# Seven block products for four of the eight row tiles of the output projections behind the feed-forward

## What is computed

```
def second_block(x, ...):
    for i in range(4):                 # mla, swa, fox, mla
        o = attention_i(x)             # 512 x 1024, 16 heads of 64
        y = (o * silu(gate)) @ w_out[i]            # 1024 x 1024
        x = layernorm(8 ** 0.25 * x + y, ln_g[i], ln_b[i])
    return x
```

## Time and profile before

| | |
|---|---|
| median of 3 runs | 1786.05 us (1785.99 to 1786.71) |
| profiled execution | 1786.31 us, its span 1784.5 us |
| granted TensorE clock | 0.998 in the mean |
| DMA | 147.94 MB, 83 GB/s |

### The profile page before, as it was taken

The page is one execution under the profiler, slowest core; times in us unless marked ns, Lnnn a source line. Parts: engine busy times, 40 slices in busy tenths (PEclk is TensorE's granted clock), DMA queues, the critical chain, the costliest instruction groups (busy, mean ns, idle before and its releaser), DMA issues.

```text
span 1784.5 us, 24874 instructions
## 1 busy us (share of the span) xinstructions
PE 1763.0 (99%) x9776; PEld 1416.5 (79%) x9776; DVE 992.6 (56%) x2091; ACT 810.8 (45%) x1737; POOL 727.3 (41%) x441
## 2 busy tenths in 40 slices
PE   9999999999999999999999999999999999999997
PEld 6787877788888888889776798888877777887676
DVE  4558688564351524254777368755644342567764
ACT  5434455453342323244476344554345343446662
POOL 4534521154686868633312333234332324332122
PEclk9999999999999999999999999999999999999999
DMA  5322320153505151324212232113331222421212
GB/s 170 99 74 71 95 60 25 36 177 92 169 25 176 36 165 48 97 74 105 61 35 82 85 99 71 60 62 96 104 87 56 74 69 84 104 68 37 61 55 72
DMA packets 215032, 147.94 MB, mean 83 GB/s; under 512 B 51825, under 2 KB 197249, under 8 KB 214914
## 3 DMA queue, kind: packets, MB, share of 16 engines
q1 hardware_dynamic: 210592, 137.10, 27.2%
q10 hardware_dynamic: 4322, 9.24, 1.5%
HBM read 144.22 MB, written 2.10 MB: 82 GB/s over the span
## 4 chain that ended last, share of the span: by engine, by line
PE 89%; DVE 7%; ACT 3%; issue 1%; DMA 0%; POOL 0%; SPq 0%; DVEq 0%; ACTq 0%
PE PS L427 24%; PE PS L429 23%; PE PS L428 23%; PE PS L515 6%; PE PS L577 6%; PE PS L601 4%; PE PS L779 1%; DVE PS L1645 1%; ACT X L1172 1%; DVE X L1648 1%; DVE PS L1664 1%; PE PS L1033 1%; PE PS L802 1%; ACT Wh L1113 0%; PE PS L1054 0%
## 5 line engine op out<-in xcount | busy, mean ns | idle before, releaser
L2291 POOL TENSOR_TENSOR Wl<-Wr,Wh 128x1024 fp32r<-128x1024 f32 (+3 forms) x367 | 600.9, 1657 | 1005.4 <-ACT Wh L1113 1005.1
L427 PE MATMUL PS<-XTl,Wh 128*128 128x512 f32 (+1 forms) x1096 | 412.9, 377 | 1.0 <-DVE KF L1683 0.8
L429 PE MATMUL PS<-XTh,Wh 128*128 128x512 f32 (+1 forms) x1096 | 408.1, 372 | 0.0
L428 PE MATMUL PS<-XTh,Wl 128*128 128x512 f32 (+1 forms) x1096 | 408.0, 372 | 0.0
L1113 ACT CAST Wh<-Wr 128x1024 fp32r<-128x1024 f32 (+5 forms) x274 | 249.3, 931 | 156.9 <-PE PS L429 95.7
L427 PEld LDWEIGHTS PS<-XTl,Wh 128*128 128x128 f32 x1096 | 206.5, 188 | 45.5 <-issue 9.9
L429 PEld LDWEIGHTS PS<-XTh,Wh 128*128 128x128 f32 x1096 | 206.4, 188 | 36.4
L428 PEld LDWEIGHTS PS<-XTh,Wl 128*128 128x128 f32 x1096 | 206.5, 188 | 34.8
L427 PE MATMUL PS<-Wl,XTh 128*128 128x512 f32 (+2 forms) x608 | 227.3, 374 | 2.1 <-DVE XTl L1656 1.5
L429 PE MATMUL PS<-Wh,XTh 128*128 128x512 f32 (+2 forms) x608 | 224.1, 369 | 0.0
L428 PE MATMUL PS<-Wh,XTl 128*128 128x512 f32 (+2 forms) x608 | 223.9, 368 | 0.0
(11 more groups left out here) (342 smaller groups left out, 2749.5 us busy)
## 6 DMA issues: line engine op xcount, KB each, us to landing
Wr<-in_w_in SPq DMA_DIRECT2D x38, 512.0 KB, 3.8
Wr<-in_fox_w_in SPq DMA_DIRECT2D x32, 512.0 KB, 4.2
Wr<-in_w_ffn_gate SPq DMA_DIRECT2D x22, 512.0 KB, 4.2
Wr<-in_w_ffn_up SPq DMA_DIRECT2D x22, 512.0 KB, 4.0
Wr<-in_swa_w_in SPq DMA_DIRECT2D x20, 512.0 KB, 4.0
WP<-in_w_ffn_down SPq DMA_DIRECT2D x9, 1024.0 KB, 9.2
Wr<-in_mla_w_in SPq DMA_DIRECT2D x16, 512.0 KB, 4.2
Wr<-in_mla_w_out SPq DMA_DIRECT2D x16, 512.0 KB, 3.4
```

The costliest lines, as they stand in the source:

```text
L427: pe.matmul(o, l[0], r[1], start=start, stop=False, skip_group_check=again)
L428: pe.matmul(o, l[1], r[0], start=False, stop=False, skip_group_check=again)
L429: return pe.matmul(o, l[0], r[0], start=False, stop=stop, skip_group_check=again)
L2291: ins = raw.tensor_tensor(l[:, cs], r[:, cs], h[:, cs].bitcast(F), sub)
```

## The change

In all four stages the row tiles 0 to 3 of the output projection, as two pairs q = 0, 1 (row tiles 2q and 2q + 1), are multiplied in another way, after Strassen and Winograd. A pair is a product of a 2 x 2 block matrix of gated tiles (rows 0 to 255 and 256 to 511, two row tiles) with a 2 x 2 block matrix of weights (two row tiles, two halves of columns). It is made of seven block products in place of eight; each block product is two (v = 0, 1) for two tiles of rows, so 14 products by `mm3` and not 16.

- Weights (`sums7`, on GpSimd, ahead of the piece "even" in its order of pieces): four sums of 128 x 512. Pieces of a stage are now, in this order, even0, sums0, even1, sums1, odd0, fours (for both pairs), odd1, and row tiles 4 to 7 as they are: 11 in place of 8. ("Even" is the even row tile, its right half replaced by a sum; "sums" and "fours" are sums.) The odd row tile is loaded twice, once for the sums and once as a piece of its own: 10 loads in place of 8. ScalarE's wait for "even", "sums" and "fours" is a wait for GpSimd's sums.
- Factors (`factors`, ScalarE and VectorE): the tiles 2q, 2q + 1 of `GT` give seven factors of 128 x 256, three as they are and four sums, which VectorE makes; they are split into `FS`, 256 + 512 + 1024 columns. It stands at the step ("gate", x), with x by SEVENS: 5 and 6 in the MLA stages, 3 and 5 in fox, 2 and 4 in swa. In MLA and fox `FS` lies over buffers that are no longer needed by then. The tiles 0 to 3 are no longer split at the stage's end; "out" is left for 4 to 7.
- Products (`outproj7`): four of the seven products have banks of their own in the first pass (A, B, C, E, each for v = 0, 1; 48 matmuls for both pairs). VectorE adds each to the rows and halves of X that it belongs to (`combine`: A and B to three places, C and E to one; A's scale the residual on the way), and the second pass (36 matmuls) goes on in the banks A, C and E, where a sum started. Then the row tiles 4 to 7 follow as before, i by i, in the same banks (B's start anew). mla1 has the same order as the others.
- The ring of raw slots takes the odd row tile as an entry of its own, which is free again when GpSimd has made the fourth sum.
- At the event ("fu", 21), the last upward product of the feed-forward, two more pieces are due.

```diff
+SEVENS = {'swa': (2, 4), 'fox': (3, 5), 'mla0': (5, 6), 'mla1': (5, 6)}
...
-            if kind == "odd":
+            if kind == "odd" and c not in SEVENS:
                 return pair_in[q].at(c)
-            if kind == "ring":
+            if kind in ("ring", "odd"):
                 return raw_in[ring[i] % RAW_SLOTS].at(i)
-            return by_pool.at(kind, c, min(2 * q + 1, PAIRS - 1) if kind == "fours" else q)
+            return by_pool.at(kind, c, min(2 * q + 1, (2 if c in SEVENS else PAIRS) - 1) if kind == "fours" else q)
+        def released(entry):
+            if entry in odd_of:
+                return by_pool.at("fours", *homes[odd_of[entry]][1:])
+            return weight_lo.at(entry)
...
-                    due[signal, key] = min(count[0] + AHEAD + (key[:2] == ("swa", 1)), len(used) + W_SLOTS)
+                    due[signal, key] = min(count[0] + AHEAD + (key[:2] == ("swa", 1)) + 2 * (key == ("fu", 21)), len(used) + W_SLOTS)
...
+                        ring["odd", i] = len(ringed)
+                        ringed.append(("odd", i))
                 return i
...
+            def outproj7(s, src, lhs, ready, turned=True):
+                A, B, C, E = ([take(("y", s, v + i, c)) for v in range(2)] for i, c in ((0, 0), (2, 1), (0, 1), (2, 0)))
+                place = {(v + i, c): bs[v] for bs, i, c in ((A, 0, 0), (B, 2, 1), (C, 0, 1), (E, 2, 0)) for v in range(2)}
+                FS = O7[s][0]
+                def row(a):
+                    return [(src[:, a:a + 1, :], 0)]
+                def product(bs, v, w, h, j, q, start, stop, again=False):
+                    e.wait_ge(weight_lo.at(w), *free(bs[v]), by_dve.at("fs", s, q))
+                    return mm3(PS[bs[v]][:, :], [t[:, q, j, tile(v)] for t in FS], part(w, 0, D, 512 * h, 512 * h + 512), start, stop, again)
+                for q in range(2):
+                    w2 = weight(row(2 * q), D, ("even", s, q))
+                    odd_src[w2] = row(2 * q + 1)
+                    w13 = weight(row(2 * q), D, ("sums", s, q))
+                    for bs, w, h, j, x in ((A, w2, 0, 0, "A"), (B, w2, 1, 5, "B"), (C, w13, 0, 4, "C"), (E, w13, 1, 3, "E")):
+                        for v in range(2):
+                            ins = product(bs, v, w, h, j, q, q == 0, q == 1)
+                            if q:
+                                ins.then_inc(*done(psum_full, "part", s, x, v))
+                        if h:
+                            if not q:
+                                ins.then_inc(*weight_used.next())
+                            used[w] = psum_full.now() if q else weight_used.now()
+                for q in range(2):
+                    wo = weight(row(2 * q + 1), D, ("odd", s, q))
+                    if q == 0:
+                        w4 = weight(row(0), D, ("fours", s, 0))
+                    for bs, w, h, j, x in ((A, wo, 0, 1, "A"), (C, wo, 1, 6, "C"), (E, w4, q, 2, "E")):
+                        for v in range(2):
+                            e.wait_ge(by_dve.at("part", s, x, v))
+                            ins = product(bs, v, w, h, j, q, False, False, again=True)
+                        if h:
+                            ins.then_inc(*weight_used.next())
+                            used[w] = weight_used.now()
+                ws = [(weight(row(a), D), a) for a in range(4, 8)]
+                for i in range(NT):
+                    for c in range(2):
+                        b, fresh = place[i, c], i >= 2 and c == 1
+                        if fresh:
+                            e.wait_ge(by_dve.at("part", s, "B", i - 2))
+                        for w, a in ws:
+                            e.wait_ge(weight_lo.at(w), *ready(a))
+                            ins = mm3(PS[b][:, :], pair(lhs, ALL, a, tile(i)), part(w, 0, D, 512 * c, 512 * c + 512), fresh and a == 4, a == 7, again=not fresh)
+                            if i == NT - 1 and c == 1 and a < 7:
+                                ins.then_inc(*weight_used.next())
+                                used[w] = weight_used.now()
+                        ins.then_inc(*done(psum_full, "y", s, i, c))
+                        give(b, (by_dve, ("normed", s, i, c)))
+                    if turned and i in (1, 2):
+                        turn_tile(s, i - 1)
+                used[ws[-1][0]] = psum_full.at("y", s, NT - 1, 1)
...
+            def factors(s, q):
+                FS, _, _, S4 = O7[s]
+                g = GT[s][:, 2 * q:2 * q + 2, :].rearrange("p f (a t) -> p (f a) t", a=2)
+                e.wait_ge(by_dve.at(s, "o", 2 * q + 1), *overlaid(s, q))
+                high(FS[0][:, q, 0, :], g[:, 0, :], "fs_hi", s, q)
+                high(FS[0][:, q, 1:3, :], g[:, 2:4, :], "fs_hi", s, q)
+                e.wait_ge(by_dve.at("sf", s, q))
+                high(FS[0][:, q, 3:7, :], S4[:, :, :], "fs_hi", s, q)
...
+                    elif kind == "gate" and x in SEVENS.get(s, ()):
+                        factors(s, SEVENS[s].index(x))
+                    elif kind == "out" and (x >= 4 or s not in SEVENS):
                         gated(s, x)
...
+                for x in "ACEB":
+                    for v in range(2):
+                        b, low, right = bank[("y", s, *{"A": (v, 0), "B": (v + 2, 1), "C": (v, 1), "E": (v + 2, 0)}[x])][:, :], X[:, v + 2, HALVES[0]], X[:, v::2, HALVES[1]]
+                        e.wait_ge(psum_full.at("part", s, x, v), by_dve.now())
+                        if x in "AB":
+                            scale = ALPHA if x == "A" else 1.0
+                            ve.scalar_tensor_tensor(low, low, scale, b, mult, add).then_inc(*by_dve.next())
+                            ve.scalar_tensor_tensor(right, right, scale, b.unsqueeze(1).broadcast_to([128, 2, 512]), mult, sub).then_inc(*by_dve.next("part", s, x, v))
+                        else:
+                            y = X[:, v + 2, HALVES[1]]
+                            ve.tensor_tensor(y, y, b, add if x == "C" else sub).then_inc(*by_dve.next("part", s, x, v))
+                e.wait_ge(by_dve.now())
             def norm_tail(s, alpha=ALPHA, x_ready=lambda i: None):
+                if s in SEVENS:
+                    combine(s)
                 for i in range(NT):
...
+            def factors(s, q):
+                FS, _, _, S4 = O7[s]
+                g = GT[s][:, 2 * q:2 * q + 2, :].rearrange("p f (a t) -> p (f a) t", a=2)
+                e.wait_ge(by_dve.now(), *([by_act.at("fs_hi", s, q - 1)] if q else []), *overlaid(s, q))
+                ve.tensor_tensor(S4[:, 0, :], g[:, 0, :], g[:, 1, :], sub).then_inc(*by_dve.next())
+                ve.tensor_tensor(S4[:, 1, :], g[:, 1, :], g[:, 3, :], sub).then_inc(*by_dve.next())
+                e.wait_ge(by_dve.now())
+                ve.tensor_tensor(S4[:, 2, :], S4[:, 1, :], g[:, 0, :], sub).then_inc(*by_dve.next())
+                e.wait_ge(by_dve.now())
+                ve.tensor_tensor(S4[:, 3, :], S4[:, 2, :], g[:, 2, :], add).then_inc(*by_dve.next("sf", s, q))
+                e.wait_ge(by_act.at("fs_hi", s, q), by_dve.now())
+                low(FS[1][:, q, 0, :], g[:, 0, :], FS[0][:, q, 0, :], "fs", s, q)
+                low(FS[1][:, q, 1:3, :], g[:, 2:4, :], FS[0][:, q, 1:3, :], "fs", s, q)
+                low(FS[1][:, q, 3:7, :], S4[:, :, :], FS[0][:, q, 3:7, :], "fs", s, q)
...
+            def sums7(i, s, q):
+                slots = [ring[x] % RAW_SLOTS for x in (i, ("odd", i))]
+                w, o = (Wr[x] for x in slots)
+                t, f = O7[s][1][:, :, :].rearrange("p (a b) n -> p a (b n)", a=2), O7[s][2]
+                e.wait_ge(raw_in[slots[0]].at(i), raw_in[slots[1]].at("odd", i), *([weight_lo.at(at_home["sums", s, 0])] if q else [by_dve.at("fs", s, 1)] if s == "swa" else []))
+                raw.tensor_tensor(t[:, 0, :], w[:, HALVES[0]], w[:, HALVES[1]], add).then_inc(*by_pool.next())
+                raw.tensor_tensor(t[:, 1, :], w[:, HALVES[1]], o[:, HALVES[1]], add).then_inc(*by_pool.next("sums", s, q))
+                e.wait_ge(by_pool.now())
+                raw.tensor_tensor(w[:, HALVES[1]], t[:, 0, :], o[:, HALVES[1]], add).then_inc(*by_pool.next("even", s, q))
+                e.wait_ge(by_pool.now())
+                raw.tensor_tensor(f[:, q, :], w[:, HALVES[1]], o[:, HALVES[0]], add).then_inc(*by_pool.next("fours", s, q))
```

More of the change, by code:

```diff
@@ L1547, in scalar @@
                             *by_act.next("turned", s, x, u, 0))
-                elif kind == "out":
+                elif kind == "gate" and x in SEVENS.get(s, ()):
+                    factors(s, SEVENS[s].index(x))
+                elif kind == "out" and (x >= 4 or s not in SEVENS):
                     gated(s, x)
@@ L2119, in mla @@
                         gate_values(s, x)
-                    elif kind == "out":
+                        if x in SEVENS.get(s, ()):
+                            factors(s, SEVENS[s].index(x))
+                    elif kind == "out" and (x >= 4 or s not in SEVENS):
                         gated(s, x)
```

67 lines of the change are left out of this document (49 added, 18 removed).

## The result

The changed kernel takes 1828.1 us (median; the kernel before 1786.4 beside it): 1.0228 of the time before, interval [1.0216, 1.0241]. The forecast was 1801.7 us, and at most 1811. The sign was right, the size was not: 26.4 us are missing from the sum.

What follows compares the result with a forecast made beforehand. TensorE was taken as the bound, busy 1763 of 1784.5 us. Terms: -2.6 (feed-forward) + 6.2 (mla0) + 1.5 (swa) + 1.0 (fox) + 6.1 + 3.5 (mla1) = +15.7, giving 1801.7 us on the median; range 1786 to 1811.

Steps and rivals of the forecast that it cites:

- Feed-forward: At ("fu", 21), two more pieces rounded there remove TensorE's wait of 2.61 us: -2.6 us.
- 2.72 us are saved as matmuls and given back as a wait for GpSimd: Each stage's opening, from the projection's first matmul (S) to y(0,1) full: still 27.2 us, no gain.
- S+4.8: Openings: GpSimd's row of eight pieces starts 3.7 us plus a cast of 1.1 after the projection's first matmul (S).
- The MLA hold: MLA stages: even0's cast waits for GpSimd's sums, holding ScalarE's copies of pair 5; with what follows, S 6.1 us later.
- TensorE wants the copies at 966.78: MLA hold: TensorE needs pair 5's copies then, transposes pair 6 at 971.2 instead of 969.09: +2.1 us.
- After gate 6 the same again: MLA stages, second factors: VectorE's operations stretch beside GpSimd; pair 7's values start about 993.5 instead of 990.8.
- swa, +1.5: swa: factors add 4.4 us into a VectorE gap of 3.7, sums run beside its scaling: +1.5 us, bounds 0 and 4.
- The end of mla1: mla1's opening and tail: y(0,1) at S+27.3 against S+23.2, span end at S+56.9 against S+53.4: +3.5 us.
- Rival C: MLA second factors: each of seven VectorE operations waits out a GpSimd sum, 7 us more a stage: 1816 us; chance 0.06.
- A: Whole kernel: GpSimd keeps up and holds are covered, so the saved work arrives: -12.9, 1773 us; chance 0.14.
- B: Openings as forecast, but the holds in the MLA stages stay hidden: 1789 us; chance 0.20.
- D: Holds are real, openings gain half, 1.4 us each: 1796 us; chance 0.60 together with the forecast.

Runs made afterwards that it cites:

- e1_due: Kernel before with only the feed-forward's due changed, two more pieces rounded at ("fu", 21): 1783.5 us, ratio 0.9980.
- e3: Kernel before with nine dummy copies on ScalarE ahead of its copies of turn 5 in the two MLA stages: 1796.6 us, ratio 1.0056.
- e5: Kernel after with GpSimd's weight sums left out in all four stages (8 columns each, product not the projection): 1804.5 us, ratio 1.0098.
- e9_slots: Kernel after with sums1 and odd0 due earlier, at values of head pair 7, and E's products first in the second round: 1819.0 us, ratio 1.0184.
- v1_fox: Kernel before with the change in fox alone, the feed-forward's due and two more pieces due at values of head pair 7: 1788.9 us, ratio 1.0012.
- e7_zero: Kernel after with nine matmuls by a tile of zeros in each of the four openings: 1825.0 us, ratio 1.0215.
- v2_fox: Kernel before with the change in fox alone, the feed-forward's due, two early pieces and gate 7 ahead of VectorE's low parts: 1787.7 us, ratio 1.0005.

## Why the prediction was wrong

**Feed-forward** -2.6: right, -2.5 (e1_due).

**"2.72 us are saved as matmuls and given back as a wait for GpSimd"**: right in all four stages, by the matmuls and by the waits for `Wl` ahead of the first y. The step that failed was the start of GpSimd's row in fox, S+4.8 by my sum (3.7 and a cast of 1.1) and S+6.9 in the profile. Its two parts:

```profile
1510.74 1.04 ACT L1209 CAST Wh<-Wr 128x1024 fp32r<-128x1024 f32 x1 [5.15 <-POOL Wr L2440]
...
1512.92 3.26 DVE L1809 TENSOR_TENSOR XTl<-GT,XTh 128x512 fp32r<-128x512 f32 x3
1516.10 0.68 DVE L1878 SCALAR_TENSOR_TENSOR GT<-GT,PS 128x512 f32<-128x512 f32 x1
...
1518.74 1.05 ACT L1209 CAST Wh<-W 128x1024 fp32r<-128x1024 f32 x1
```

even1's cast waits 5.15 us for its sums, so the low parts start at S, where they started a microsecond ahead of it; then three of them take 3.26 us beside the split of even1, where 1.9 would do. I had counted them at the duration of the earlier trace rows, taken when GpSimd was idle. 2.1 us for the start and at most 1.7 for the clock make up the 3.7. In mla0 the row starts at S+3.9 (1003.21), loses 0.8 waiting for the last row tile's cast and has that tile split at S+23.7, forecast S+23.8; its excess of 1.5 is the clock.

**The MLA hold**: its place and its 5.8 us were right. The step that failed is "TensorE wants the copies at 966.78", which is 963.3 on after's time scale: it wanted their banks at 960.8, for the scores of pair 7. I followed who reads the copies and not who takes the bank. The hold alone costs 5 (e3), not 2.1.

**"After gate 6 the same again", the second factors**: named at the right place. I allowed about 2 us for stretching from the mean of the earlier trace rows; the mean hides that an operation that starts beside GpSimd waits for its whole instruction. In after it met three of the seven, 4.3 us for 1.3. S came 13.1 and 12.7 us later in the two stages instead of 6.1. The waits themselves were not so far off: I had 3.3 up to the first factors and 2.8 for the second, and by the matmuls TensorE stands 4.1 and 3.7 us in mla0. The larger miss is the half clock behind them, 6.8 and 4.5 us of it up to S with TensorE busy, which cost at most 5.6 us.

**swa, +1.5**: the worst term, 10.5. I set 4.4 us of factors against a gap of 3.7 seen on VectorE, as if its idle time stood where the factors go, and gave ScalarE's casts nothing; the queries of the next scores stand behind these casts, so each factor block shows (2.7 us for two). 3.23 us was in the rows and I used it once; with sums there are two at 5.2, and TensorE waits for each of them. That accounts for what e5 left and what it took, with the clock; the part of the casts is read from the trace and not tried.

**The end of mla1**, +3.5: it was 1.3. y(0,1) came 0.9 sooner than I had it (S+26.7), and the tail, which I took from fox, 1.3 shorter (27.9 us). This and the -1.0 ahead of 770 went the other way and hide 3 us of the misses.

**The clock**: no term at all. It is at most 18.8 us of the 41.8. The run with zeros prices a stretch of 3.4 us at 1.5 to 2.1 us.

**Rival C** had the mechanism: the Trainium skill, page "SBUF — State Buffer", section "🔬 SBUF: two separate sides", says that the shared port pair is held for a whole instruction and the other engine fully blocks. The trace agrees: 2.43 us a low part beside pieces of 2.4, against 0.69 alone. I gave it 0.06 because a mean of 1954 ns looked mild. Its price was not right either: in MLA three operations of the seven were held and not all, about 3 us and not 9, and its figure of 1816 falls 12 short, since it has neither the clock nor swa. A and B are refuted, D too: no opening gained.

## What to carry to other kernels

Ask of each new wait on TensorE what the granted clock does behind it, and add that to the wait. Ask of each held copy who takes its bank next, not only who reads it. Ask of each new cast what stands behind it in its engine's order. And give VectorE's two-input SBUF operations, and its scaling of tiles in SBUF, the price of a whole GpSimd instruction wherever both may run, instead of a mean; a change that gives GpSimd more work has to find that work a place where VectorE has none of those.

## What the runs showed of the hardware

- Waits of TensorE of 2.4 us (mla0's opening) and of 1.8 and 1.6 us (swa's) come with 3.4 us at a granted clock of 0.5, in the wait or up to 1.1 us behind it; mla1's longest, 1.9 us, came with none. A wait of 3.6 us in fox came with 6.8 us at 0.5 in e9_slots and with none in v1_fox's profiled execution. Where the stretch falls seems to bear on its price: swa's attention came out at 186.8 or 188.4 us with the same code in it. Why it falls in one place or the other was not tried.
- Matmuls by a tile of zeros in TensorE's waits kept the clock at 1.00 in three openings where it had been 0.93 to 0.95 (e7_zero).
- VectorE's low parts of 512 columns take 0.69 us alone and 2.43 to 2.55 in the mean beside a row of GpSimd pieces (v2_fox, v1_fox); GpSimd's pieces stretch from 2.40 to 2.86 in turn. VectorE's additions with one operand in PSUM kept their 0.69 and 1.22 in the same stretch.
